# One decay row spread over 128 partitions by TensorE instead of by DMA, in a hybrid encoder layer

## The reference

```python
# gated DeltaNet, 6 heads: G is the running sum of log decays in a chunk
decay = jnp.exp(jnp.where(incl, G[..., :, None] - G[..., None, :], -jnp.inf))
L = jnp.where(strict, jnp.einsum('nbhtd,nbhsd->nbhts', kb, kc) * decay, 0.0)
T = lax.linalg.triangular_solve(L, eye, left_side=True, lower=True, unit_diagonal=True)
a_intra = jnp.einsum('nbhtd,nbhsd->nbhts', qc, kc) * decay

# mLSTM, 4 heads
D = jnp.where(incl, b[..., :, None] - b[..., None, :] + ic[..., None, :], -jnp.inf)
W = jnp.exp(D_i - m_t[..., None]) * s_i
num = (w_inter[..., None] * jnp.einsum('bhtd,bhde->bhte', q_i, C)
       + jnp.einsum('bhts,bhse->bhte', W, v_i))
```

## Time and profile before

| | |
|---|---|
| median of the runs | 2064.64 us |
| the profiled execution | 2064.64 us, its span 2062.8 us |
| PE busy | 2030.2 us, 98% of the span |
| DVE busy | 1219.1 us, 59% |
| ACT busy | 892.3 us, 43% |
| POOL busy | 27.6 us, 1% |
| DMA | 378.75 MB, 184 GB/s over the span |

### The profile page before, as it was taken

One profiled execution on the slowest core, in us unless ns is written; L12 is line 12 of the kernel. 1 busy time (PEld: TensorE's weight loads), 2 busy tenths in 40 slices (PEclk: granted clock), 3 DMA queues, 4 the chain that ended last, 5 costly groups with the idle time before them and its releaser, 6 DMA issues.

```text
span 2062.8 us, 36597 instructions
## 1 busy us (share of the span) xinstructions
PE 2030.2 (98%) x15772; PEld 1963.9 (95%) x15772; DVE 1219.1 (59%) x1322; ACT 892.3 (43%) x869; POOL 27.6 (1%) x47
## 2 busy tenths in 40 slices
PE   7999999999999999999999999999999999999998
PEld 7999999999999999999999999888888888999998
DVE  5677643544544467576565345677778778744443
ACT  4445333434355433455444334544444444433332
POOL 0000000000000000000000000000000000000000
PEclk9999999999999999999999999999999999999999
DMA  8566434565556856556555355656556556556664
GB/s 262 167 200 194 138 113 155 165 199 169 167 170 217 295 176 220 176 179 190 174 194 163 124 160 175 215 185 203 177 189 199 177 194 195 182 179 201 192 187 127
DMA packets 354751, 378.75 MB, mean 184 GB/s; under 512 B 7887, under 2 KB 350707, under 8 KB 353363
## 3 DMA queue, kind: packets, MB, share of 16 engines
q1 hardware_dynamic: 350659, 353.36, 54.0%
q0 software_dynamic: 3984, 23.74, 3.1%
HBM read 366.06 MB, written 11.02 MB: 183 GB/s over the span
## 4 chain that ended last, share of the span: by engine, by line
PE 94%; DVE 2%; ACT 2%; issue 1%; DMA 0%; POOL 0%; SPq 0%; DVEq 0%; ACTq 0%
PE bank L1793 22%; PE bank L1795 21%; PE bank L1794 21%; PE bank L1827 15%; PE bank L1829 8%; PE bank L2004 1%; DVE w_lo L1029 1%; PE bank L1959 1%; ACT w_hi L479 1%; PE bank L2201 1%; PE bank L2182 1%; ACT x_home L479 0%; PE bank L1864 0%; DMA ident<-in_shape_masks 0%; PE bank L1953 0%
## 5 line engine op out<-in xcount | busy, mean ns | idle before, releaser
L1029 DVE TENSOR_TENSOR w_lo<-raw,w_hi 128x2048 fp32r<-128x2048 f32 (+1 forms) x353 | 765.8, 2170 | 624.3 <-ACT w_hi L479 624.1
L479 ACT ACTIVATE w_hi<-raw 128x2048 fp32r<-128x2048 f32 (+2 forms) x355 | 644.4, 1816 | 1094.2 <-PE bank L1795 819.3
L1793 PE MATMUL bank<-x_home,w_hi 128*128 128x256 f32 x2304 | 648.8, 282 | 5.5 <-DVE w_lo L1029 2.5
L1794 PE MATMUL bank<-x_home,w_hi 128*128 128x256 f32 x2304 | 643.2, 279 | 0.0
L1795 PE MATMUL bank<-x_home,w_lo 128*128 128x256 f32 x2304 | 642.7, 279 | 0.0
L1827 PE MATMUL bank<-x_home,w_hi 128*128 128x512 f32 x1408 | 488.7, 390 | 3.6 <-DVE x_home L1675 2.2
L1793 PEld LDWEIGHTS bank<-x_home,w_hi 128*128 128x128 f32 x2304 | 433.1, 188 | 7.5 <-DVE w_lo L1029 2.3
L1794 PEld LDWEIGHTS bank<-x_home,w_hi 128*128 128x128 f32 x2304 | 433.2, 188 | 0.2
L1795 PEld LDWEIGHTS bank<-x_home,w_lo 128*128 128x128 f32 x2304 | 433.1, 188 | 0.0
L1829 PE MATMUL bank<-x_home,w_lo 128*128 128x256 f32 x1408 | 397.0, 282 | 0.0
L1827 PEld LDWEIGHTS bank<-x_home,w_hi 128*128 128x128 f32 x1408 | 264.2, 188 | 60.0 <-DVE xT L1043 1.7
(11 more groups left out here) (295 smaller groups left out, 2139.2 us busy)
## 6 DMA issues: line engine op xcount, KB each, us to landing
raw<-in_w_in SPq DMA_DIRECT2D x52, 2048.0 KB, 8.5
raw<-in_ffn_up SPq DMA_DIRECT2D x44, 2048.0 KB, 8.0
raw<-in_ffn_down SPq DMA_DIRECT2D x32, 1408.0 KB, 6.4
raw<-in_xa_wkv SPq DMA_DIRECT2D x16, 2048.0 KB, 9.1
raw<-in_w_br SPq DMA_DIRECT2D x8, 2048.0 KB, 8.5
raw<-in_w_out SPq DMA_DIRECT2D x8, 2048.0 KB, 8.2
raw<-in_xa_wq SPq DMA_DIRECT2D x8, 2048.0 KB, 8.1
raw<-in_xa_wo SPq DMA_DIRECT2D x8, 2048.0 KB, 8.1
```

The lines of the kernel that those rows point to most:

```text
L479: return nc.scalar.activation(out_, in_, func, **kw)
L1029: tt(split_out(w_lo, kind, half), halves(raw, kind, half, par), split_out(w_hi, kind, half).bitcast(f32), ALU.subtract).then_inc(lo_ready, 1)
L1793: mm(o, w[0], x[0], start=start, stop=False)
L1794: mm(o, w[0], x[1], start=False, stop=False)
```

## The change

The rows no longer go through DRAM. Where a head's row is wanted on 128 partitions, PE multiplies it with a column of the identity: the stationary operand is `ident[0:n, h:h+1]`, repeated to n x 128, the moving one the row tile (n x 256), so each of 128 partitions of the PSUM output gets row h. n is 6 for `g_row` and 4 for `m_row`, and the operands are f32. This is done 6 times before the first decays, 6 times again before the second, and once for each mLSTM head. DVE then reads the row from PSUM.

```diff
-            pool.wait_ge(row_v, ROW_V)
-            pool.dma_start(row_spill[0:GH, :], g_row[:, :]).then_inc(rows, 16)
-            pool.dma_start(row_spill[GH:GH + MH, :], m_row[:, :]).then_inc(rows, 16)
-            pool.wait_ge(rows, 32)
-            pool.wait_ge(tm_t, 9)
-            pool.dma_start(g_rows, row_spill[0:GH, :].unsqueeze(0).to_broadcast([P, GH, SEQ])).then_inc(rows, 16)
...
-            pool.wait_ge(a_v, 12)
-            pool.dma_start(m_rows, row_spill[GH:GH + MH, :].unsqueeze(0).to_broadcast([P, MH, SEQ])).then_inc(rows, 16)
...
-            beside(m + 3)
-            dve.wait_ge(rows, 48)
-            for h in range(GH):
-                for a in range(TT):
-                    v.tensor_scalar(S_L[:, a * GH + h, :], g_rows[:, h, a * P:(a + 1) * P],
-                                    cols[:, a, 32 + h:33 + h], 0.0, ALU.subtract, ALU.max).then_inc(dec_v, 1)
+            for j in range(3):
+                dve.wait_ge(dec_t, j + 1)
+                for x in range(2):
+                    for a in range(TT):
+                        h = 2 * j + x
+                        v.tensor_scalar(S_L[:, a * GH + h, :], mb6(j + 3)[:, x * SEQ + a * P:x * SEQ + a * P + P],
+                                        cols[:, a, 32 + h:33 + h], 0.0, ALU.subtract, ALU.max).then_inc(dec_v, 1)
+            beside(m + 3)
             beside(m + 4)
...
+            for j in range(3):
+                dve.wait_ge(a_t, j + 1)
+                for x in range(2):
+                    for a in range(TT):
+                        h = 2 * j + x
+                        av(v.tensor_scalar(S_L[:, a * GH + h, :], bank[4 + j][:, x * SEQ + a * P:x * SEQ + a * P + P],
+                                           cols[:, a, 32 + h:33 + h], 0.0, ALU.subtract, ALU.min))
...
             for g in range(3):
-                dve.wait_ge(a_t, 1 + g)
+                dve.wait_ge(a_t, 4 + g)
...
             def ml_weights(h):
-                b = bank[5 + 2 * ML_PAIR[h]]
-                v.scalar_tensor_tensor(ml_x[:, h, 0:SEQ], m_rows[:, h, :], cols[:, 0, 96 + h:97 + h], pos_mask[:, 0:SEQ],
+                b = bank[4 + 2 * ML_PAIR[h]], bank[5 + 2 * ML_PAIR[h]]
+                dve.wait_ge(ml_s, h + 1)
+                v.scalar_tensor_tensor(ml_x[:, h, 0:SEQ], b[0][:, 0:SEQ], cols[:, 0, 96 + h:97 + h], pos_mask[:, 0:SEQ],
                                        ALU.subtract, ALU.add).then_inc(ml_v, 1)
-                v.scalar_tensor_tensor(ml_x[:, h, SEQ:384], m_rows[:, h, P:SEQ], cols[:, 1, 96 + h:97 + h], pos_mask[:, SEQ:384],
+                v.scalar_tensor_tensor(ml_x[:, h, SEQ:384], b[0][:, P:SEQ], cols[:, 1, 96 + h:97 + h], pos_mask[:, SEQ:384],
                                        ALU.subtract, ALU.add).then_inc(ml_v, 1)
                 dve.wait_ge(ml_a, h + 1)
-                dve.wait_ge(ml_s, h + 1)
-                v.scalar_tensor_tensor(ml_x[:, h, :], b[:, 0:384], DK ** -0.5, ml_x[:, h, :], ALU.mult, ALU.mult).then_inc(ml_w, 1)
+                v.scalar_tensor_tensor(ml_x[:, h, :], b[1][:, 0:384], DK ** -0.5, ml_x[:, h, :], ALU.mult, ALU.mult).then_inc(ml_w, 1)
...
             dve.wait_ge(mask_in, 32)
-            dve.wait_ge(rows, 64)
...
+            def spread(b, h, row):
+
+                n = row.shape[0]
+                return mm(b, ident[0:n, h:h + 1].to_broadcast([n, P]), row, start=True, stop=True)
...
             tm_transposes(range(6, 9))
+            pe.wait_ge(tm_ed, 3)
+            pe.wait_ge(tm_ea, 3)
+            for j in range(3):
+                for x in range(2):
+                    last = spread(mb6(j + 3)[:, x * SEQ:(x + 1) * SEQ], 2 * j + x, g_row[:, :])
+                last.then_inc(dec_t, 1)
             product_half(m + 2)
             product_half(m + 3)
...
             for g in range(6):
+                if g == 3:
+                    pe.wait_ge(dec_v, 12)
...
             pe.wait_ge(qd_e, 2)
+            for j in range(3):
+                for x in range(2):
+                    last = spread(bank[4 + j][:, x * SEQ:(x + 1) * SEQ], 2 * j + x, g_row[:, :])
+                last.then_inc(a_t, 1)
             chunk_pairs(a_t, (bank[7], bank[2], bank[3]), 0)
             product_half(m + 2)
+            pe.wait_ge(a_v, 8)
...
             def ml_scores(h):
+                spread(bank[4 + 2 * ML_PAIR[h]][:, 0:SEQ], h, m_row[:, :])
                 scores(bank[5 + 2 * ML_PAIR[h]], qk_b[:, MH + h, :], qk_b[:, h, :]).then_inc(ml_s, 1)
```

More of the change, by code:

```diff
@@ L219, in build_program @@
         x_spill = nc.dram_tensor("x_spill", [P, KC * SEQ], f32).ap()
-        row_spill = nc.dram_tensor("row_spill", [GH + MH, SEQ], f32).ap()
-        g_rows, m_rows = conv[:, 12:12 + GH, :], conv[:, 12:12 + MH, :]
         g_spill = nc.dram_tensor("g_spill", [P, (GA_UNITS + GB_UNITS) * 2 * SEQ], f32).ap()
@@ L262, in build_program @@
         set_up = sem("set_up")
-        rows = sem("rows")
         gw_h, gw_l, row_mm, row_v, row_a, row_t, col_e, col_a = (sem(n) for n in (
@@ L269, in build_program @@
             "conv_v", "conv_silu", "tm_t", "tm_ea", "tm_ed", "l2_v", "l2_a", "qk_t", "qk_e", "kv_v", "qd_t", "qd_e"))
-        dec_v, dec_a, kk_t, l_v, z_t, z_e, d_t, d_e, c_v = (sem("gdn_" + n) for n in (
-            "dec_v", "dec_a", "kk_t", "l_v", "z_t", "z_e", "d_t", "d_e", "c_v"))
+        dec_t, dec_v, dec_a, kk_t, l_v, z_t, z_e, d_t, d_e, c_v = (sem("gdn_" + n) for n in (
+            "dec_t", "dec_v", "dec_a", "kk_t", "l_v", "z_t", "z_e", "d_t", "d_e", "c_v"))
         u_t, u_e, w_t, w_e, s_t, s_e, a_t, a_v, a_a, vn_t, vn_e, o_t, o_e, yn_v, yn_a, y_t, y_e = (sem("gdn_" + n) for n in (
```

## The result

The changed kernel takes 2075.65 us (median of four runs, 2074.88 to 2077.14), the kernel before 2064.60 us beside it (2063.21 to 2064.74). The ratio is 1.0058, with a 95% interval of 1.0046 to 1.0069: slower by 11 us. The forecast was 2073.4 us in a range of 2069.5 to 2077, with 2071.5 to 2075.5 as the likeliest part. Further executions on record (26) lie between 2074.00 and 2079.18 us, with a median of 2076.3. The profiled execution took 2076.52 us, with a span of 2074.7 us against 2062.8.

What follows compares the result with a forecast made beforehand. PE was taken as the bound: 6.9 us of spreads, 1.0 of shape switches, 0 at the decays, 0.7 and 0.2 of waits at mLSTM heads, 8.8 us on 2064.64, giving 2073.4 us; range 2069.5 to 2077.

Steps and rivals of the forecast that it cites:

- PE is the bound, and what goes is worth 0: Whole kernel: PE limits the time; the removed writes, broadcasts and DVE waits free no wait of PE, so 0 us.
- Sixteen spreads, 6.9 us: On PE: 16 f32 products of 256 columns at 0.431 us each, priced by a row of that width and type.
- The cheap rival: On PE: a product of few rows costs only 0.15 us, switch included; 3.8 us in all, 2068.4 us; chance 7%.
- the dear one: On PE: repeated-column loads or the switch prevent overlap, 0.76 us a spread, 12.2 us plus waits, 2077.8 us; chance 9%.
- Six trips, 1.0 us: On PE: six changes to the small array shape and back, 0.17 us each, at two spread groups and four mLSTM heads.
- its upper bound: Shape changes on PE: if all of the largest step, 0.26 us, were switch, twice that a trip, 3.1 us in all.
- The forecast's test of a PE gap: On PE: a gap of 0.1 to 0.2 us at the ends of each run of spreads would show the shape changes.
- First and second decays, 0: DVE's decays reading PSUM, 3.2 us for twelve, stay hidden behind PE's work at both places: no loss.
- the margin of 0.6 us: First decays: w_lo reaches PE at about 196.8, PE wants it at 197.4, so the slower decays cost nothing.
- Waits at heads 0/1 and 2: 0.7 and 0.2 us: mLSTM heads: PE waits for w_lo, delayed by the DVE and ACT chain after the spreads: 0.7 us, then 0.2 us.
- the forecast's own formula: Heads 0 and 1: PE's wait is 0.90 us less one shape switch of 0.17 us, giving 0.7 us.

Runs made afterwards that it cites:

- interleaved: Changed kernel with the first group's six spreads put singly between slices of the following half, the second group's in twos between chunk pairs: 2077.29 us, ratio 1.0064.
- high and low rows: Changed kernel with rows as rounded high and low parts, one fp32r product per spread, mLSTM spreads a half early: 2066.11 us, ratio 1.0008.
- the last version: The version with high and low rows, with DVE's old order at the first decays, the w_lo half ahead of the twelve decays: 2067.35 us, ratio 1.0021.

## Why the prediction came out right

**PE is the bound, and what goes is worth 0.** Shown: the kernel before with the spreads alone added is as slow as the kernel after, up to the 0.7 us of the waits at the heads.

**Sixteen spreads, 6.9 us.** Inside the row of six spreads the step is 0.433 us, as in the row of 256 columns, so six rows cost what 128 do. The cheap rival, argued from the earlier trace rows, is out; so is the dear one.

**Six trips, 1.0 us.** The mechanism was right and the size was not. The trips of the kernel after take 0.37 and 0.39 us at the groups, and 0.39, 0.39, 0.39 and 0.40 at the heads, 2.3 in all; interleaved they cost 0.39 and 0.40 each. The estimate had taken 0.17 from two four-row transposes, which have four columns each; its upper bound (the largest step is all switch, twice 0.26) was nearer. The rule of the Trainium skill that the forecast cites (TensorEngine Tiling (Array Packing), Key Properties: a change of tiling mode drains TensorE) names no price; the trips of 0.37 to 0.40 us agree with it.

**The clock, not in the sum.** This is the term that was missing: 1.65 us in the profiled execution, 3.3 in one with a fall at both groups. Of the profiles with groups of at most 32 rows in a row, nine of twelve groups have a slow stretch behind them; of those with 64 or 128 rows, with spreads between other products, or with fp32r spreads, none of the 14. The single spreads of four rows at the heads have none either. The forecast's test of a PE gap would not have found it, since PE never stops in the records.

**First and second decays, 0.** Right, and for the reason given. With rows on 128 partitions and no fall of the clock the transposes begin here:

```profile
194.90 2.79 PE L1986 MATMUL bank<-ident,proj 128*128 128x128 f32 x24
```

PE wants the `w_lo` at 194.90 + 24 x 0.106 = 197.4, and it is done at 196.8: the margin of 0.6 us that was forecast. With high and low rows, where PE comes 2.1 us earlier (192.76), it waits for this `w_lo`.

**Waits at heads 0/1 and 2: 0.7 and 0.2 us.** 0.44 and 0.17 by the starts (and 0.07 more for the slower first product behind the second), and both gone when the spreads stand a half earlier. The trip of 0.39 instead of 0.17 us delays PE twice and DVE's chain only once, so the forecast's own formula, 0.90 us less a trip, gives 0.5 for the first; with 128 rows, where there is no trip, it is 0.73 by the record and 0.82 by the starts.

**The sum.** 6.9 + 2.3 + 1.65 + 0.7 = 11.5 us in place of 8.8. The result, +11.0, is just above the likeliest part of the forecast and lies in the upper third of the range, which had been put there for dear spreads. That is luck in part: the reason for it was another. Of the 2.7 us that the sum lacked, the clock is 1.65 and the trips 1.3, and the waits give 0.2 back.

What stays open is why the clock falls at a row of few-row products, and why not every time. The runs show which versions have the fall and which do not, not the mechanism.

## What to carry to other kernels

In a kernel whose queue on PE is full, a broadcast by products costs its products, even if it saves a round trip through DRAM: ask first who waited for the transfer, and if nobody did, leave it. If it has to be on PE, give it the shape and the type of the products around it (here 128 rows and fp32r parts: 2.8 us by the starts and 1.2 by the medians for the 16 spreads and their waits, instead of 11). And when a product is priced by a row of the same width, look up its number of rows as well: the width gave the step right, the rows brought a trip and a slower clock.

## What the hardware showed

- A row of f32 products on six or 32 rows, 256 columns, 2.8 to 6.5 us long, was followed in nine of twelve cases by 3.0 to 4.9 us at the lower clock level (products 0.213 us apart instead of 0.117), with PE busy in every record before it; with 128 rows it was in none of six, with 64 rows in none of two.
- Idle time of PE brought the lower clock in some places and not in others: at a wait of 3.52 us late in the program all 14 profiles have it, behind a wait of 1.3 to 2.3 us at 15 us four of the 14, and behind the wait of 2.39 us of the last version there is none.
- Changing between few and 128 rows and back costs 0.37 to 0.40 us, for six rows as for 64: against the same row of products on 128 rows both take 0.38 us more.
- A stationary operand that is one column repeated 128 times loads like any other: 0.79 / 6 = 0.13 us a product in fp32r, beside 0.117 for the products of the weight halves.
- DVE's twelve decays of 128 columns take 3.19 us with the rows in PSUM, 2.44 with them in SBUF.
